# Block inverse of the gated delta rule: four of six turns as full-size transposes of two heads each, products on crossed halves of the array

## What is computed

```
def chunk_gated_delta_rule(q, k, v, g, beta):
    ...
    a_mat = jnp.where(strict, kk * decay * beta[..., :, None], 0.0)
    lhs = jnp.eye(CHUNK, dtype=jnp.float32) + a_mat
    rhs = jnp.concatenate([v * beta[..., None], k * (beta * jnp.exp(G))[..., None]], axis=-1)
    sol = lax.linalg.triangular_solve(lhs, rhs, left_side=True, lower=True, unit_diagonal=True)
    ...
```

## Time and profile before

| | |
|---|---|
| median of 3 runs | 2650.03 us (2649.62 to 2650.58) |
| the profiled execution's own time | 2650.27 us |
| its span in the profile | 2648.5 us |
| PE busy | 2623.4 us, 99% |
| DVE, ACT, POOL busy | 1499.0, 1456.2, 849.7 us |

### The profile page before, as it was taken

How to read it: one execution, slowest core, us unless ns; L and a number is a source line. 1 busy time by engine, 2 the same in 40 slices (tenths; PEclk the granted TensorE clock), 3 DMA queues, 4 the chain that set the end, 5 groups by cost and what they waited for, 6 DMA issues and landing times.

```text
span 2648.5 us, 45346 instructions
## 1 busy us (share of the span) xinstructions
PE 2623.4 (99%) x16762; PEld 2282.7 (86%) x16762; DVE 1499.0 (57%) x2457; ACT 1456.2 (55%) x2146; POOL 849.7 (32%) x443
## 2 busy tenths in 40 slices
PE   9999999999999999999999999999999999999999
PEld 8888998888888998888889999988888899999887
DVE  5543645546543645546556787355455567873654
ACT  5445665445545655445455845664455558456643
POOL 0007672000017675000008754810100186548100
PEclk9999999999999999999999999999999999999999
DMA  7655446555555446656667742566565586325664
GB/s 225 185 180 180 141 155 190 184 191 183 184 180 174 144 160 193 188 183 192 186 163 182 162 88 79 175 189 187 178 197 187 155 192 159 81 81 182 188 187 143
DMA packets 351973, 447.17 MB, mean 169 GB/s; under 512 B 32446, under 2 KB 241344, under 8 KB 351776
## 3 DMA queue, kind: packets, MB, share of 16 engines
q1 hardware_dynamic: 350032, 442.80, 56.7%
q10 hardware_dynamic: 816, 1.21, 0.1%
q0 software_dynamic: 928, 0.45, 0.1%
HBM read 443.31 MB, written 1.05 MB: 168 GB/s over the span
## 4 chain that ended last, share of the span: by engine, by line
PE 94%; ACT 4%; DVE 2%; issue 1%; DMA 0%; SPq 0%; DVEq 0%; ACTq 0%
PE PS L522 29%; PE PS L524 28%; PE PS L523 28%; PE PS L725 1%; ACT wh L547 1%; PE PS L1109 1%; PE PS L1182 1%; PE PS L1172 1%; PE PS L691 1%; PE PS L1049 1%; PE PS L913 1%; PE PS L960 0%; DVE PS L2299 0%; ACT xh L1319 0%; PE PS L826 0%
## 5 line engine op out<-in xcount | busy, mean ns | idle before, releaser
L547 ACT ACTIVATE wh<-ring 128x1024 fp32r<-128x1024 f32 (+2 forms) x840 | 883.7, 1054 | 875.0 <-PE PS L522 867.7
L555 POOL TENSOR_TENSOR wl<-ring,wh 128x1024 fp32r<-128x1024 f32 (+2 forms) x332 | 785.7, 2382 | 1603.7 <-ACT wh L547 1603.2
L555 DVE TENSOR_TENSOR wl<-ring,wh 128x1024 fp32r<-128x1024 f32 x508 | 621.7, 1226 | 612.1 <-ACT wh L547 612.0
L522 PE MATMUL PS<-wh,xh 128*128 128x512 f32 (+2 forms) x1760 | 692.3, 393 | 1.3 <-DVE xl L1921 1.1
L524 PE MATMUL PS<-wh,xl 128*128 128x512 f32 (+2 forms) x1760 | 682.5, 388 | 0.0
L523 PE MATMUL PS<-wl,xh 128*128 128x512 f32 (+2 forms) x1760 | 681.3, 387 | 0.0
L522 PE MATMUL PS<-xh,wh 128*128 128x256 f32 x1536 | 447.9, 292 | 0.1
L524 PE MATMUL PS<-xh,wl 128*128 128x256 f32 x1536 | 434.3, 283 | 0.0
L523 PE MATMUL PS<-xl,wh 128*128 128x256 f32 x1536 | 434.2, 283 | 0.0
L522 PEld LDWEIGHTS PS<-wh,xh 128*128 128x128 f32 x1760 | 330.7, 188 | 68.9 <-issue 3.9
L524 PEld LDWEIGHTS PS<-wh,xl 128*128 128x128 f32 x1760 | 330.4, 188 | 68.5
(11 more groups left out here) (318 smaller groups left out, 2468.5 us busy)
## 6 DMA issues: line engine op xcount, KB each, us to landing
ring<-in_ffn_w_in_dram SPq DMA_DIRECT2D x352, 256.0 KB, 3.0
ring<-in_mix_w_in_dram SPq DMA_DIRECT2D x256, 256.0 KB, 3.7
ring<-in_ffn_w_gate_dram SPq DMA_DIRECT2D x176, 256.0 KB, 2.8
ring<-in_ffn_w_up_dram SPq DMA_DIRECT2D x176, 256.0 KB, 3.0
ring<-in_ffn_w_down_dram SPq DMA_DIRECT2D x176, 256.0 KB, 2.8
ring<-in_w_in_dram SPq DMA_DIRECT2D x176, 256.0 KB, 2.9
ring<-in_ffn_w_out_dram SPq DMA_DIRECT2D x176, 256.0 KB, 2.8
ring<-in_w_branch_dram SPq DMA_DIRECT2D x32, 256.0 KB, 2.9
```

The costliest lines, as they stand in the source:

```text
L522: first_ = mm(o, w[0], x[0], start=start, stop=False, skip_group_check=True)
L547: act_(dst, src, ACT.Copy).then_inc(hi_ready, 1)
L555: (engine or v_).tensor_tensor(dst, src, part_views(t, wh)[0], ALU.subtract).then_inc(lo[t.slot()], 1)
```

## The change

Levels 2 to 5 only, so `tr1` to `tr4`:

- `tr` is now `turn_pairs`: for each chunk two transposes of 128x128, each of two neighbouring heads over both halves. A transpose of [128 tokens, (2 heads, 64)] puts the first head's blocks on partitions 0 to 63 and the second's on 64 to 127, with the half of the tokens as the column block. So in `Uc` the heads lie crossed: head h of half b is now on the half h % 2, column block 2 (h // 2) + b.
- `m` writes crossed to match: input rows of half b, output on half h % 2, and in bank 2 + 2c + b, at column 320. So it uses all four quarters of the array.
- `pt` reads on half h % 2 and writes on half r, in bank 2 + 2c + h % 2, at column 256: again all four quarters. (At level 1 it still reads and writes half r, but in the new banks.)
- ACT copies `m` from two banks in one instruction, and it now waits for `tr{l-1}.c` ahead of `mc{l}.c`, since `m` now writes into `tr`'s bank.
- DVE's `T` at levels 1 to 5 is two instructions of 128x64 elements in place of one of 128x128.

`tr0`, `tr5`, `m6` and `pu6` stay as they are.

```diff
+M_AT, PT_AT = 320, 256
...
+            def turn_pairs(l, c, src):
+
+                for p in range(2):
+                    ins = nc.tensor.transpose(bank(3 + 2 * c, p * P, (p + 1) * P),
+                                              src[c][:, 2 * p:2 * p + 2, :].rearrange("p h n -> p (h n)"), ident)
+                did(ins, f"{g}.tr{l}.{c}")
+
...
                         for h in range(4):
-                            for r in half:
-                                o = PS[r, 2 + 2 * c, h * 32:(h + 1) * 32].rearrange("p (i y) -> p i y", y=1 << l)
-                                ins = mm(o, alc[c][r, h, :], lower(Tc[c][r, h, :], l), start=True, stop=True)
+                            for b, r in enumerate(half):
+                                if l == 1:
+                                    o = PS[r, 2 + 2 * c, h * 32:(h + 1) * 32]
+                                else:
+                                    o = PS[half[h % 2], 2 + 2 * c + b, M_AT + h // 2 * 32:M_AT + (h // 2 + 1) * 32]
+                                ins = mm(o.rearrange("p (i y) -> p i y", y=1 << l), alc[c][r, h, :],
+                                         lower(Tc[c][r, h, :], l), start=True, stop=True)
                         did(ins, f"{g}.m{l}.{c}")
                         if l > 1:
-                            turn(l - 1, c, Tc)
+                            turn_pairs(l - 1, c, Tc)
...
                         for h in range(4):
-                            for r in half:
-                                ins = mm(PS[r, 2 + 2 * c, S + h * 32:S + (h + 1) * 32], Uc[c][r, h, :], m1n[c][r, h, :],
-                                         start=True, stop=True)
+                            for b, r in enumerate(half):
+                                if l == 1:
+                                    at, i = r, h
+                                else:
+                                    at, i = half[h % 2], 2 * (h // 2) + b
+                                o = PS[r, 2 + 2 * c + h % 2, PT_AT + h // 2 * 32:PT_AT + (h // 2 + 1) * 32]
+                                ins = mm(o, Uc[c][at, i, :], m1n[c][at, i, :], start=True, stop=True)
                         did(ins, f"{g}.pt{l}.{c}")
...
                         wp(f"{g}.m{l}.{c}")
-                        act_(m1n[c], blocks(2 + 2 * c, 32), ACT.Copy).then_inc(dl[1].sem, dl[1].did(f"{g}.mc{l}.{c}"))
                         if l > 1:
                             wp(f"{g}.tr{l - 1}.{c}")
+                        if l == 1:
+                            ins = act_(m1n[c], blocks(2 + 2 * c, 32), ACT.Copy)
+                        else:
+                            ins = act_(m1n[c].rearrange("p (i b) n -> p b i n", b=2),
+                                       PS[:, 2 + 2 * c:4 + 2 * c, M_AT:M_AT + 64].rearrange("p b (i n) -> p b i n", i=2), ACT.Copy)
+                        ins.then_inc(dl[1].sem, dl[1].did(f"{g}.mc{l}.{c}"))
+                        if l > 1:
                             act_(Uc[c], blocks(3 + 2 * c, HD), ACT.Copy).then_inc(dl[1].sem, dl[1].did(f"{g}.U{l - 1}.{c}"))
...
                         if l < 6:
-                            T = lower(Tc[c].rearrange("p h n -> p (h n)"), l)
                             wp(f"{g}.pt{l}.{c}")
-                            part = bank(2 + 2 * c, S, S + P).rearrange("p (i y) -> p i y", y=1 << l)
-                            did(tt(T, T, part, ALU.subtract), f"{g}.T{l}.{c}")
+                            w = 1 << l
+                            T = Tc[c].rearrange("p (i b) (k y) -> p b i k y", b=2, y=2 * w)[:, :, :, :, 0:w]
+                            part = PS[:, 2 + 2 * c:4 + 2 * c, PT_AT:PT_AT + 64].rearrange("p b (i k y) -> p b i k y", i=2, y=w)
+                            for i in range(2):
+                                ins = tt(T[:, :, i], T[:, :, i], part[:, :, i], ALU.subtract)
+                            did(ins, f"{g}.T{l}.{c}")
```

## The result

| | before | after |
|---|---|---|
| median of 20 runs each | 2650.05 us (2649.62 to 2650.58) | 2654.34 us (2651.52 to 2655.27) |
| the profiled execution's own time | 2650.27 us | 2654.79 us |
| its span, mean granted TensorE clock | 2648.5 us, 1.000 | 2653.1 us, 0.994 |

The ratio is 1.0013, 95% interval 1.0007 to 1.0019: 4.3 us slower, where the forecast had 5.2 us faster. The time lies outside the range (2643.2 to 2651.6). In the terms of the prediction that is "within 0.2%", but the sign is wrong and the cause isn't one that it names.

The account below looks back on a forecast made before the run. PE, busy 99%, bounds the kernel. Per layer 1.86 us (filled levels), 0.49 (group 0, levels 4 and 5) and 0.37 (group 1, levels 3 to 5) make 2.7; two layers 5.4, less 0.2: 2644.8 us, range 2643.2 to 2651.6.

Parts of the forecast that it names:

- The crossed groups: m and pt, levels 2 to 5: 16 records on four quarters at once take 0.23 us in place of 0.46.
- The switch: Between quarter-size products and full-size transposes: 0.15 us extra, so tr.0 follows m.0 by 0.38 us.
- ACT's new order: After a turn, ACT does mc.1 and then U.1, so pt.1 loads 2.23 us into the level, before at 2.62.
- Two `T` at 0.13 spacing: DVE's T as two 64-element instructions 0.13 us apart: +0.07 us for a chunk, +0.12 for a level.
- A: Rival for m and pt: only two quarters work at a time, level 3.31 us, kernel 2651.5 us; chance 0.18.
- B: Rival for m and pt: instruction issue limits a group to some 0.30 us, kernel 2646.7 us; chance 0.15.
- C: Rival for pt: same-row records hold up the queue, a group takes 0.93 us, kernel 2661 us; chance 0.06.
- D: Rival for the turns: switches cost less than at tr0, 0.45 us more saved per filled level, kernel 2640.3 us; chance 0.04.
- A level: Level of the inverse followed by a fill: 2.62 us in place of 3.24, so 0.62 saved.
- the whole: Gain over both layers: 2.7 us per layer, 5.4 in all, 5.2 after 0.2 off for the fourth quarter.
- Nothing downstream should take it back: Behind the inverses: DVE waits 4.0 us for PE at group 1's start, ACT and POOL mostly idle, so the gain stays.
- PE idle 0.5 us in each level: Ahead of pt.1 PE waits about 0.5 us for ACT's U.1.

Follow-up runs that it names:

- e12: The changed kernel with fills spread ahead of pt, as halves in group 0 and quarters in group 1, other engines' steps moved to match; 2638.64 us.
- e13: The changed kernel plus 22 useless fill-size products per layer where PE waits, in levels 4 and 5 of group 0 and 3 to 5 of group 1; 2645.72 us.
- e1: The changed kernel with turns 1 to 4 made by eight crossed quarter-size products each instead of full-size transposes; 2648.21 us.
- e2: The kernel before with turns 1 to 4 as two full-size transposes per chunk, m and pt left on diagonal quarters (timing only); 2654.25 us.
- e3: The changed kernel with DVE's convolution steps redistributed among the levels, same total; 2655.77 us.
- e9: The changed kernel plus 39 useless fill-size products per layer, at levels 4 and 5 of group 0 and 3 to 5 of group 1; 2648.86 us.
- e11: The changed kernel plus useless fill-size products in group 1 only, 22 per layer; 2650.38 us.

## Why the prediction was wrong

*Right.* The crossed groups: 0.23 us forecast, and 0.56 - 0.33 = 0.23 between two of them in e12. The switch: `m.0` to `tr.0` 0.37, forecast 0.38. ACT's new order: `pt.1` 2.30 behind `m.0`, forecast 2.23. Two `T` at 0.13 spacing: four in a row take 0.61 us in the kernel after, and one of that size 0.22, so (0.61 - 0.22) / 3. Rivals A, B and C are out by the first of these, D by the second. The rule that A names, from the Trainium skill's page "TensorE: Matmul & The Clock Gate", Part 3, The mechanism, doesn't hold for these products: quarters of the same rows overlap. Of the 32 records in 0.56 us, 16 are on each half of the rows, and one behind another at 0.058 they would take 0.93.

*Off in size.* A level 2.69 instead of 2.62, and the whole 4.5 instead of 5.2 (e13, extra products included).

*Wrong.* The step "Nothing downstream should take it back". The sum has no term for the clock, and it measured 8.8 us. The step looked at the waits of DVE, ACT and POOL and took PE's own rate as given, at the level that the earlier trace rows happen to have. Its list of what would make it wrong has no line on the clock either. Yet it forecast PE idle 0.5 us in each level and longer ahead of level 5 and `m6`, and products put in just these waits hold the clock (e13). The time lost is 8.8 us (e13's gain of 4.5 and the change's loss of 4.3) for 27.3 us at the half clock. PE working all the time would lose half of them, 13.6; it also waits there, and I take it that waiting costs the same at either clock.

*What stays open.* What exactly the chip looks at. A stretch of 6 us with PE busy for 4.45 was followed by a fall (after), one with 4.48 was not (e1, 1558 to 1564 us), and one with 6.00 was (e2). e3 held in one layer and fell in the other. No column of the profile orders the cases. That the fall of the clock is what costs, and that PE having too little to do over the unfilled levels brings it about, is shown by e9, e11 and e13, in both directions; how light is too light isn't. Nor does every execution fall alike: the change's 20 runs spread over 3.8 us, the kernel before's over 1.0. How much of e2's 4.2 us belongs to the switches and how much to its 13.6 us at the half clock wasn't separated.

## What to carry to other kernels

Where a change takes work from an engine that is counted as 99% busy, look at what the clock does in the stretches that become light, a few microseconds at a time; the page's mean hides it. When dependent small products get shorter, move the independent work between them with them, in smaller pieces: the same change was 4.3 us slower with the old placement and 11.4 us faster with quarter fills. A test that adds useless work to the light stretch separates the clock from waits and switches, since neither lets the kernel get faster by it. Before a run is read as "fewer waits", look in its trace whether they are fewer.

## What the runs showed of the hardware

Four quarters of the array load and multiply at once: 32 records of 64x64 in 0.56 us, 0.0144 us for a further one on average, where two quarters take 1.01 us. Full-size transposes between quarter-size products cost 0.14 us at the switch (0.37 from `m.0` to `tr.0`, less 0.23), even with crossed products ahead of them.

The granted clock fell to its half level without any long wait: the longest beside a fall in the change's first layer were 0.99 and 1.05 us, with PE counted busy for 74 to 84% of the 6 us before. The page "TensorE: Matmul & The Clock Gate" of the Trainium skill, Part 1, HAM oscillation, tells of loops that fall because PE waits for a DMA in each turn; here dependent products with short waits were enough, which is nearer to its next section, "A second HAM failure mode", on frequent short pauses.
